# A two-block transformer kernel on one core: products of a chunked recurrence in column tiles of 64, values of a sparse attention in pairs, decay rows of an attention as two rounded parts

## What is computed

```
# first block, recurrence: one step per position
sa = einsum('bhvk,bhk->bhv', state, a_t)
state = state * w_t + sa * b_t + v_t * k_t
y_t = einsum('bhvk,bhk->bhv', state, r_t)
# first block, sparse attention: values
o_lat = einsum('bqhk,bqkc->bqhc', p, lat_sel)
o = einsum('bshc,chd->bshd', o_lat, w_uv)
# second block, attention with decay
c = cumsum(log_sigmoid(f_logit), axis=1)
s = einsum('bhqd,bkhd->bhqk', q, k) * scale
s = s + c[t] - c[s_]      # row terms c[t] drop out of the softmax
p = softmax(where(s_ <= t, s, -inf))
```

## Time and profile before

| | us |
|---|---|
| median of three runs | 1311.58 |
| lowest, highest | 1308.89, 1313.55 |
| profiled execution, its own time | 1307.0 |
| its span | 1305.2 |

### The profile page before, as it was taken

One profiled execution on the slowest core, in us unless ns is written; L12 is line 12 of the kernel. 1 busy time (PEld: TensorE's weight loads), 2 busy tenths in 40 slices (PEclk: granted clock), 3 DMA queues, 4 the chain that ended last, 5 costly groups with the idle time before them and its releaser, 6 DMA issues.

```text
span 1305.2 us, 20923 instructions
## 1 busy us (share of the span) xinstructions
PE 1196.7 (92%) x8244; PEld 1006.2 (77%) x8244; DVE 465.2 (36%) x833; ACT 593.9 (46%) x869; POOL 906.7 (69%) x913
## 2 busy tenths in 40 slices
PE   2998999999898999998989889989979989999997
PEld 2898988786577888788968767767769977888785
DVE  6476446644443111004255654332234133111101
ACT  2464133236445454435444354554456444554532
POOL 0688335424395888785999983668869757888784
PEclk9999799999999999999999998999999999999998
DMA  8655223333554556564655442435646534555562
GB/s 327 199 153 171 57 61 112 99 98 98 156 166 147 184 186 184 175 189 113 184 156 138 136 133 81 123 103 182 191 128 185 170 97 146 180 187 182 170 200 82
DMA packets 182914, 196.74 MB, mean 151 GB/s; under 512 B 7416, under 2 KB 141856, under 8 KB 182688
## 3 DMA queue, kind: packets, MB, share of 16 engines
q1 hardware_dynamic: 178336, 186.62, 47.1%
q10 hardware_dynamic: 4480, 8.78, 2.1%
HBM read 194.31 MB, written 1.06 MB: 150 GB/s over the span
## 4 chain that ended last, share of the span: by engine, by line
PE 73%; POOL 9%; DVE 7%; issue 5%; ACT 4%; DMA 1%; POOLq 0%; ACTq 0%; SPq 0%; DVEq 0%
PE ps L632 20%; PE ps L634 19%; PE ps L633 19%; PE ps L629 13%; POOL wlo L2473 9%; PE ps L637 3%; DMA raw<-in_ada_w 1%; DVE hE L1737 1%; ACT whi L1216 1%; DVE gt L1737 1%; DVE x L1745 0%; ACT L1216 0%; DVE acc L1745 0%; DVE gab L1737 0%; ACT gt L1216 0%
## 5 line engine op out<-in xcount | busy, mean ns | idle before, releaser
L2473 POOL TENSOR_TENSOR wlo<-raw,whi 128x256 fp32r<-128x256 f32 (+1 forms) x904 | 901.2, 1030 | 381.8 <-ACT whi L1216 379.6
L1216 ACT ACTIVATE whi<-raw 128x1024 fp32r<-128x1024 f32 x325 | 341.3, 1056 | 318.8 <-PE ps L634 307.3
L632 PE MATMUL ps<-whi,hThi 128*128 128x512 f32 (+2 forms) x672 | 270.4, 402 | 10.7 <-POOL wlo L2473 5.2
L634 PE MATMUL ps<-whi,hTlo 128*128 128x512 f32 (+2 forms) x672 | 261.0, 388 | 0.0
L633 PE MATMUL ps<-wlo,hThi 128*128 128x512 f32 (+2 forms) x672 | 260.3, 387 | 0.0
L632 PE MATMUL ps<-hThi,whi 128*128 128x256 f32 x576 | 170.9, 297 | 11.0 <-issue 4.2
L633 PE MATMUL ps<-hTlo,whi 128*128 128x256 f32 x576 | 164.6, 286 | 0.0
L634 PE MATMUL ps<-hThi,wlo 128*128 128x256 f32 x576 | 164.5, 286 | 0.0
L632 PEld LDWEIGHTS ps<-whi,hThi 128*128 128x128 f32 x672 | 128.5, 191 | 43.3 <-issue 15.8
L634 PEld LDWEIGHTS ps<-whi,hTlo 128*128 128x128 f32 x672 | 128.4, 191 | 26.7
L633 PEld LDWEIGHTS ps<-wlo,hThi 128*128 128x128 f32 x672 | 128.7, 192 | 22.0
(11 more groups left out here) (362 smaller groups left out, 1556.6 us busy)
## 6 DMA issues: line engine op xcount, KB each, us to landing
raw<-in_w_in SPq DMA_DIRECT2D x121, 512.0 KB, 3.5
raw<-in_ffn_w_in SPq DMA_DIRECT2D x176, 256.0 KB, 3.0
raw<-in_ffn_w_down SPq DMA_DIRECT2D x44, 512.0 KB, 4.2
raw<-in_ada_w SPq DMA_DIRECT2D x24, 512.0 KB, 5.3
raw<-in_w_mkv SPq DMA_DIRECT2D x16, 512.0 KB, 3.7
raw<-in_w_o SPq DMA_DIRECT2D x8, 512.0 KB, 3.6
raw<-in_w_branch_a SPq DMA_DIRECT2D x8, 512.0 KB, 3.6
raw<-in_w_branch_b SPq DMA_DIRECT2D x8, 512.0 KB, 3.7
```

The costliest lines, as they stand in the source:

```text
L632: e.matmul(o, l[0], r[0], start=start, stop=False)
L634: return e.matmul(o, l[1], r[0], start=False, stop=stop)
L1216: return e.activation(o, i, f, **k)
L2473: p = e.tensor_tensor(wlo[c % NHL][:, o], raw[i % NRAW][:, o], whi[c % NHL][:, o], ALU.subtract)
```

## The change

Three parts. In the head chains every full-width product behind the solve is cut into two column tiles of 64 (r), whose outputs go to partitions 0 to 63 and 64 to 127 of the same bank; those on the state become four quadrant products per chunk; the state itself is computed for each head in its own column tile, so that VectorE scales it in one instruction; and the solve's WT and WG products alternate by head. In the sparse attention values are issued for two heads together, after heads 2, 4, 6 and at the end. In the second attention the rows are rounded to fp32r in partitions 0 to 7 and the remainder in partitions 32 to 39 of a 128-row tensor whose other rows are zero; the selector has ones in both places, and one fp32r product over 128 rows replaces the fp32 one over 8.

```diff
+        sel, lfr = Z_("sel", [P, 8, 128], F32R), Z_("lfr", [P, 256], F32R)
...
-                            m = mm(bs[i][:, 0:64], TK[:, 2 * i + c, 0, :], VT[:, c, h * 64:h * 64 + 64], True, c == 0)
+                            for r in two:
+                                m = mm(bs[i][r, 0:64], TK[:, 2 * i + c, 0, r], VT[:, c, h * 64:h * 64 + 64], True, c == 0)
                         if c == 1:
                             w.wait_ge(v_, (f, "S0"))
-                            for i in range(2):
-                                p0 = i * 64
-                                m = mm(bs[i][:, 0:64], AR[p0:p0 + 64, f, 1, 0, :], S0[p0:p0 + 64, :], False, True)
+                            for r in two:
+                                for i, q in enumerate(two):
+                                    m = mm(bs[i][r, 0:64], AR[q, f, 1, 0, r], S0[q, :], False, True)
...
                         for i in range(2):
                             mm(b[0:64, i * 64:i * 64 + 64], WT[0:64, 2 * i + c, :], XU[0:64, 0, i, :])
-                        for i in range(2):
                             m = mm(b[64:128, i * 64:i * 64 + 64], WG[:, 2 * i + c, :], XU[:, 0, i, :])
...
-                            mm(b[:, 0:128], btT[:, 0, :], XU[:, 1, :, :].rearrange("p i v -> p (i v)"), True, False)
-                            mm(b[:, 0:128], btT[:, 1, :], VT[:, 0, 2 * f * 64:(2 * f + 2) * 64], False, True).then_inc(
-                                pe.tick((f, "S")), 1)
+                            for i, q in enumerate(two):
+                                mm(b[q, 0:64], btT[:, 0, q], XU[:, 1, i, :], True, False)
+                            for i, q in enumerate(two):
+                                h = 2 * f + i
+                                m = mm(b[q, 0:64], btT[:, 1, q], VT[:, 0, h * 64:h * 64 + 64], False, True)
+                            m.then_inc(pe.tick((f, "S")), 1)
...
-                            mm(bs[i][:, 0:64], TB[:, 2 * i + c, 1, :], XU[:, 1, i, :], True, False)
-                            m = mm(bs[i][:, 0:64], TK[:, 2 * i + c, 1, :], VT[:, c, h * 64:h * 64 + 64], False, c == 0)
+                            for r in two:
+                                mm(bs[i][r, 0:64], TB[:, 2 * i + c, 1, r], XU[:, 1, i, :], True, False)
+                            for r in two:
+                                m = mm(bs[i][r, 0:64], TK[:, 2 * i + c, 1, r], VT[:, c, h * 64:h * 64 + 64], False, c == 0)
...
                 def values(h):
-                    p0 = h % 2 * 64
-                    w.wait_ge(a_, ("o", h))
-                    b = bank("side", ("ds", "y", h), "ds_v", ("y", h))
-                    mm(b[p0:p0 + 64, 0:256], wuv[:, h * 64:h * 64 + 64], olT[:, h % 2, :]).then_inc(pe.tick(("y", h)), 1)
+                    w.wait_ge(a_, ("o", h + 1))
+                    bs = [bank("side", ("ds", "y", h + i), "ds_v", ("y", h + i)) for i in range(2)]
+                    for i in range(2):
+                        p0 = i * 64
+                        m = mm(bs[i][p0:p0 + 64, 0:256], wuv[:, (h + i) * 64:(h + i) * 64 + 64], olT[:, i, :])
+                    m.then_inc(pe.tick(("y", h), ("y", h + 1)), 1)
...
-                    return mm(o, sel[:, h, :], lf[:, 3, 0:n], False, True)
+                    return mm(o, sel[:, h, :], lfr[:, 0:n], False, True)
...
-                ts(lf[:, 3, :], nc_, -1.0, None, ALU.mult).then_inc(S["ev_v"].tick("lf"), 1)
+                ts(lfr[0:8, :], nc_, -1.0, None, ALU.mult).then_inc(S["ev_v"].tick(), 1)
+                w.wait_ge(S["ev_v"])
+                stt(lfr[32:40, :], nc_, -1.0, lfr[0:8, :], ALU.mult, ALU.subtract).then_inc(S["ev_v"].tick("lf"), 1)
...
-                            for p0 in (0, 64):
-                                ts(S0[p0:p0 + 64, :], PS[bank_of[z, f, "S"]][p0:p0 + 64, p0:p0 + 64], esc[p0:p0 + 64, f:f + 1], None,
-                                   ALU.mult).then_inc(s.tick((f, "S0")), 1)
+                            ts(S0, PS[bank_of[z, f, "S"]][:, 0:64], esc[:, f:f + 1], None, ALU.mult).then_inc(s.tick((f, "S0")), 1)
...
+                zero = C("zero", 0, 1)
+                cp(sel[:, :, :], zero.unsqueeze(2).broadcast_to([P, 8, 128])).then_inc(S["ev_v"].tick(), 1)
+                cp(lfr[:, :], zero.broadcast_to([P, 256]))
+                w.wait_ge(S["ev_v"])
+                for r in (0, 32):
+                    o = CON["ident"][0] + r
+                    cp(sel[r:r + 8, :, :], con[r:r + 8, o:o + 8].unsqueeze(2).broadcast_to([8, 8, 128])).then_inc(
+                        S["ev_v"].tick("sel"), 1)
```

More of the change, by code:

```diff
@@ L525, in program @@
         Z["vb"], Z["ga"] = Z_("vb", [P, 2, 1024]), Z_("ga", [P, 8, 256])
-        lf, sel, lb = Z_("lf", [8, 4, 256]), Z_("sel", [8, 8, 128]), Z_("lb", [P, 2, 8])
+        lf, lb = Z_("lf", [8, 4, 256]), Z_("lb", [P, 2, 8])
+        sel, lfr = Z_("sel", [P, 8, 128], F32R), Z_("lfr", [P, 256], F32R)
         Z["gt"] = Z_("gt", [P, 16, 256])
@@ L950, in head @@
                             h = 2 * f + i
-                            mm(bs[i][:, 0:64], TB[:, 2 * i + c, 1, :], XU[:, 1, i, :], True, False)
-                            m = mm(bs[i][:, 0:64], TK[:, 2 * i + c, 1, :], VT[:, c, h * 64:h * 64 + 64], False, c == 0)
+                            for r in two:
+                                mm(bs[i][r, 0:64], TB[:, 2 * i + c, 1, r], XU[:, 1, i, :], True, False)
+                            for r in two:
+                                m = mm(bs[i][r, 0:64], TK[:, 2 * i + c, 1, r], VT[:, c, h * 64:h * 64 + 64], False, c == 0)
                         if c == 1:
-                            for i in range(2):
-                                p0 = i * 64
-                                m = mm(bs[i][:, 0:64], AR[p0:p0 + 64, f, 1, 1, :], S0[p0:p0 + 64, :], False, True)
+                            for r in two:
+                                for i, q in enumerate(two):
+                                    m = mm(bs[i][r, 0:64], AR[q, f, 1, 1, r], S0[q, :], False, True)
                         m.then_inc(pe.tick((f, "y", c, 0), (f, "y", c, 1)), 1)
@@ L1043, in values @@
                 def values(h):
-                    p0 = h % 2 * 64
-                    w.wait_ge(a_, ("o", h))
-                    b = bank("side", ("ds", "y", h), "ds_v", ("y", h))
-                    mm(b[p0:p0 + 64, 0:256], wuv[:, h * 64:h * 64 + 64], olT[:, h % 2, :]).then_inc(pe.tick(("y", h)), 1)
-                yield from attention("ds", logits, lambda h, k: lat[:, k, :], lambda h: values(h - 1) if h else None, *dsa_bufs[:2])
-                values(7)
+                    w.wait_ge(a_, ("o", h + 1))
[4 more added lines that the diff above has]
+                    m.then_inc(pe.tick(("y", h), ("y", h + 1)), 1)
+                yield from attention("ds", logits, lambda h, k: lat[:, k, :], lambda h: values(h - 2) if h in (2, 4, 6) else None,
+                                     *dsa_bufs[:2])
+                values(6)
                 yield
@@ L2237, in dsa, with pair @@
                 w.wait_ge(S["ev_v"], ("zb1",))
-                yield from attention("ds", lambda t: wk[t][:, :], lambda h: values(h - 1) if h else None, *dsa_bufs)
-                values(7)
+                def pair(h):
+                    if h in (2, 4, 6, 8):
+                        values(h - 2)
+                        values(h - 1)
+                yield from attention("ds", lambda t: wk[t][:, :], pair, *dsa_bufs)
+                pair(8)
                 yield
@@ L2415, in mix_start @@
                     S["pre_v"].tick("lb"), 1)
-                cp(sel[:, :, :], con[0:8, CON["ident"][0]:CON["ident"][0] + 8].unsqueeze(2).broadcast_to([8, 8, 128])).then_inc(
-                    S["ev_v"].tick("sel"), 1)
+                zero = C("zero", 0, 1)
[6 more added lines that the diff above has]
+                        S["ev_v"].tick("sel"), 1)
                 w.wait_ge(S["pre_a"], "lb")
```

## The result

| us | before | after |
|---|---|---|
| median in the first comparison | 1310.31 (4 runs) | 1292.93 (4 runs, 1288.56 to 1299.16) |
| median in a second, later one | 1311.67 (17 runs) | 1293.16 (6 runs, 1290.16 to 1300.15) |
| profiled execution, its own time | 1307.0 | 1291.93 |
| its span | 1305.2 | 1290.1 |

The ratio is 0.9879 with a 95% interval of 0.9852 to 0.9905, and 0.9878 (0.9845 to 0.991) in the second comparison. The change is faster, as forecast, but by 17.4 us and not by 10: 1292.93 lies under the range, 1296 to 1307.5. The first comparison's own runs of the kernel before have their median 1.3 us under the 1311.6 from which I forecast, so of the miss of 8.7 us, 7.4 are too small a gain.

What follows compares the result with a forecast made beforehand. TensorE, busy 1196.7 us of the span, was taken to bound the kernel. Recurrence 0, values -1.7, decay rows -8.7 and added work +0.45 gave -10.0, so a median of 1301.6 us, range 1296 to 1307.5.

Steps and rivals of the forecast that it cites:

- The values term: Sparse attention: value products issued in pairs at 0.73 us a pair, -1.7 us, bounds 0 and -2.3.
- The recurrence term: Head chains: +0.5 first u, -1.1 state and first output, -1.1 second output, -0.5 second u, +2.25 solve, together 0.
- decay rows and the wait for them: Second attention: -8.7 us for the logits, +0.45 for the extra VectorE rounding step that TensorE waits for.
- Tiles overlap: Recurrence: 64-wide column tiles sharing all rows run at once, 0.03 us an instruction; rival without overlap 1309.6 us, chance 0.07.
- my 0.058 us for an instruction with a tile to itself: Price from the solve's one-quadrant products, used as the upper bound for the new column tiles.
- Solve: Alternating WT and WG products adds two changes of form in each of 8 places, +2.25 us; cheap-or-overlapping rival, chance 0.15.
- Full-width fp32 instructions on 128 columns ... 0.10 each: Price of the recurrence's old full-width instructions, from 8 taking 0.80 us in the sparse attention's logits.
- 0.14 us for a change of form: TensorE price for each switch of tile form, taken from the solve's products and used throughout the recurrence.
- the first u: First chunk's u in the recurrence: 8 tiled instructions and two form changes replace 4 full ones, 0.12 us worse, four times.
- One product with its two changes takes 0.58 us: Sparse attention: price of one value product before the change, eight of them 4.6 us.
- Decay rows: Second attention's logits: 0.96 us less in four places with 128 keys, 1.22 in four with 256, together -8.7.
- The clock: Rival: full clock in 190 to 304 us falls to half, or the stretch behind the decay wait lengthens; slower, chance 0.06.

Runs made afterwards that it cites:

- fp32 form: Kernel before with only the decay rows changed, to 128 rows kept in fp32, a single rounded part less: 1299.12 against 1306.09 us, ratio 0.9951.
- the grouped kernel: Whole change, but the solve's products in the order of before (both of WT, then both of WG): 1290.83 us, ratio 0.9866; again 1291.14.
- the longer wait: Whole change plus four unused VectorE instructions ahead of the signal for the decay rows: 1293.08 against 1306.09 us for the kernel before, ratio 0.9909.
- the 8-row form: Kernel before with the decay rows rounded to fp32r in one part over 8 rows, remainder left out: 1303.54 us, ratio 0.9982.

## Why the forecast was right in its sign and wrong in its size

Two terms of the sum were mis-sized, and one stood at nothing. The values term, -1.7, measured -2.9 between slab products, because I priced a product from its own start and so missed what its change of form costs the block ahead. The recurrence term, 0, measured -2.4: full-width instructions cost more than the 0.10 us taken, and a change between two column forms less than 0.14. And time at half clock was not in the sum at all; the second comparison has 3.6 us less of it, which is not clear of noise. With the 1.3 us by which the runs beside the first comparison lay under my starting median, these make up the miss of 8.7: 3.7 of clock-free time (13.7 instead of 10.0), 3.6 and 1.3.

Part by part, in us, the traces' figure taken between slab products and the clock-free one from the runs with that part alone:

| part | forecast | traces | clock-free |
|---|---|---|---|
| recurrence | 0 | -2.4 | -2.6 |
| values | -1.7 | -2.9 | -3.5 |
| decay rows and the wait for them | -8.25 | -8 | -8.6 |
| whole change | -10.0 | -12.7 | -13.0 and -13.7 |

So some 3 to 4 us of the miss are mis-sized terms, all on one side. The parts add up to -14.7 clock-free, with an uncertainty of 1.3, since all three are compared with the same runs of the kernel before, and to -13.3 by the traces. That is the whole change within the uncertainty; that the parts take 1 us or so from each other is not excluded. (The traces' figure for the decay rows holds a subtraction of half-clock time, which moves it by about 0.5.)

**Tiles overlap: right.** 0.029 us an instruction against the 0.03 taken. "TensorE: Matmul & The Clock Gate" of the Trainium skill, section "The mechanism", would have it that a weight load overlaps only where the row group differs; here both column tiles share all rows, and the measurement decides against that rule for this form. By it, at my 0.058 us for an instruction with a tile to itself, these blocks would have taken twice as long.

**Solve: right.** 2.25 us laid out in the eight places, 1.96 of it in the time, with a cost seen at each boundary. The Trainium skill's page "TensorEngine Tiling (Array Packing)", section "Key Properties", has a change of tiling mode drain the engine; the trace agrees in that each change costs time, 0.14 us here, though a drain as such is not visible in it.

**"Full-width fp32 instructions on 128 columns ... 0.10 each": too low.** The timeline of the kernel before, state and first output of two pairs, first block, first block of the second pair, and the slab product behind:

```profile
198.69 0.38 PE L629 MATMUL ps<-XU,btT 128*128 128x128 f32 x2
...
199.97 0.44 PE L629 MATMUL ps<-XU,btT 128*128 128x128 f32 x2
...
201.29 0.36 PE L632 MATMUL ps<-hThi,whi 128*128 128x256 f32 x1
```

They are 24 instructions in 2.60 us, 0.108 each. The change replaces 28 full-width ones in each of four pairs, so this error is 112 x 0.008 = 0.9 us. The same step after the change:

```profile
199.31 0.34 PE L630 MATMUL ps<-XU,btT 128*64 128x64 f32 x4
...
200.86 0.39 PE L633 MATMUL ps<-hThi,whi 128*128 128x256 f32 x1
```

1.55 us, and it starts 0.08 later behind its slab product: 1.63, where 48 x 0.03 and two changes gave 1.72.

**"0.14 us for a change of form", for every change: too high between two column forms.** In the rows of the second output further up, a tiled block of four takes 0.12. From the last one to the quadrant products it takes 0.22 (209.71 - 209.49), the eight quadrant instructions take 0.28 where 8 x 0.03 is 0.24, and the first tiled block behind them 0.16 (210.15 - 209.99): 0.10, 0.04 and 0.05 over, 0.19 for going there and back where I had put 0.28. And the first u, forecast as +0.12 each, was partly in the shadow of TensorE's own wait for ScalarE (0.98 us before, 0.85 after).

**Values: the footprint of a block was the wrong measure.** "One product with its two changes takes 0.58 us": no, the change ahead of it shows in the block before, as 0.18 us more of the sums. Four blocks fewer at 0.75 are 3.0, and the second product of a pair is free, not 0.15. Both were outside my upper bound, which had four times 0.58.

**Decay rows: right as a sum, by two errors that cancel.** With 128 keys a place gives 0.95 us and 0.06 in the slab product behind (forecast 0.96), with 256 keys 1.30 and 0.11 (forecast 1.22): 9.7 us in eight places instead of 8.7. The longer wait is 0.45, as taken. But the logits now end sooner than VectorE's exchange of the row maxima: the waits for z0f grew from 0.7 to 1.6 us and gave 0.9 back. -9.7 + 0.45 + 0.9 = -8.4. I had asked what is late next for VectorE's recurrence product, but not for its softmax.

**The clock: not priced, and not settled.** In the runs of the second comparison the time fell by 17.3 us in the mean and the clock-free time by 13.7; 3.6 us, with an uncertainty of 2.0, are less time lost at half clock. The same difference is 1.7 us for the decay rows alone, 1.5 for their fp32 form, 2.8 and 3.8 for the grouped kernel, 3.4 for the longer wait, 0.2 to 0.6 for the 8-row form, the values and the recurrence alone, and 1.2 for the solve's alternation alone. Each is uncertain by 0.6 to 2.9 us, so they single out no part. In 775 to 800 us the half-clock time was 10.2, 10.2, 6.8, 6.8, 3.4 and 0 in six profiles with 8-row decay products, and 6.8, 6.8, 3.4, 3.4, 3.4, 0 and 0 in seven with full rows.

Three kernels were profiled twice, and this stretch came out alike both times: 10.2 us in the kernel before, 0 in the changed kernel, 6.8 in the grouped one. So chance in a single execution hardly explains it. But the changed and the grouped kernel have the same decay products and the same wait of 2.8 us and still differ by 6.8, so neither the form of the decay products nor the length of the wait decides it alone. What does stays open.

**The range** failed for its lower end. I gave the medians 1 to 2 us of scatter, where the kernel before moved by 5.6 between chips, all of it at an equal clock-free time, and I let the bounds of the three terms partly offset each other. They shared their faulty measure, so they erred together. Even with the measured clock-free gain, 1311.6 - 13.7 = 1297.9 would still have been 5.0 too high, about the 3.6 of the clock and the 1.3 of the median that I started from.

## What to carry to other kernels

Price a small TensorE step from the slab product ahead to the slab product behind, with and without the step, and not from its first start to the next: a change of tile form also delays the block's start, by up to 0.18 us here, and that shows only in the block before it. Count the changes of form first and the instructions second: gathering a lone 64-column product into a pair, giving an 8-row operand all 128 rows with zeros, and keeping like forms together were each worth more than the work they add. When a step gets shorter, look for what VectorE then has not finished, and compare parts of some us by span times granted clock, whose mean over 16 to 23 runs was equal within 0.6 us where medians differed by 5.6.

## What the runs showed that was not expected

- A second value product in the other column tile (two more instructions on 256 columns) adds 0.59 - 0.57 = 0.02 us.
- An fp32 product over 8 rows pays more for its form with wider operands: four changes cost 1.56 - 0.81 = 0.75 us with 128 keys and 2.40 - 1.54 = 0.86 with 256.
- Sixteen small fp32 products over 8 of 128 rows held 9.7 us of a span of 1305: with zeros in the other rows and one instruction for two, that much went.
- The kernel before loses 25.0, 26.5 or 29.9 us to half clock in the mean of its runs on three chips. Part of the pattern repeats: both its profiles have 17.1 us at half clock from 147 us on and 10.2 from 786 us on. Later stretches differ: from 800 to 1000 us there are 3.4 us of it in one profile and 13.6 in the other.
